# Sparse attention: one reciprocal for all head norms, compression at 128 rows, rows as head pairs, merge-gate products between the rows

## The chip, the cores and the metric

The kernel runs on one core of one Trainium2 chip. The metric is the device time of one execution in microseconds; the median of several runs is compared. PE is TensorE, DVE is VectorE, ACT is ScalarE, POOL is GpSimd, SP is SyncE, which here only issues the weight transfers.

## The reference, cut to what matters

The whole network has four transformer layers (latent attention, stick-breaking attention, retention, latent attention, each with a feed-forward part), and then one block of sparse attention with a layer of retrieved experts. The sequence has 512 tokens, the model 1024 features, everything in float32. The change touches only the sparse attention (stage "nsa"):

```
h = rms_norm(x, norm1);  z = h @ w_in
q (8 heads x 64), kc vc ks vs kw vw (2 groups x 64 each), gates, dil (3 groups x q,k,v x 4 heads x 64), mg (2 x 1024)
q, ks, kw, dil q, dil k: rms_norm over each head's 64 features, times a gain, then rotation of 16 of them
k_cmp, v_cmp = gelu(blocks(kc or vc, 32 tokens, stride 16) + pe) @ w1) @ w2      # 31 compressed tokens
per head: softmax over the compressed tokens, over the selected tokens, over a window;
          o = g0 * o_c + g1 * o_s + g2 * o_w
dilated: per head three patterns share one softmax over 3 x n keys
merged = sigmoid(mg[0]) * (y_nsa @ w_up_nsa) + sigmoid(mg[1]) * (y_dil @ w_up_dil);  x += merged @ w_o
```

At 512 tokens all key blocks are selected and the window covers all earlier tokens, so that the kernel computes both branches as causal attention.

## The kernel before, in words

Activations lie with features on the 128 partitions and 512 tokens along them. All weights come in one stream of slots of 128 x 1024 float32 (512 KB), through a ring of four: SP loads a slot when PE has released the one four before it (L351), ACT scales it in place and writes its float16 high half (L989, L992), POOL writes the low half (L438). ACT does that two slots ahead of what it evacuates (`feed`, `use`, L994 to L1006). An f32 product by weights is three f16 matmuls: high x high, high x low, low x high (`split_tile`, L486). One output tile of 128 features is one slot, 24 matmuls of 512 columns. Its PSUM bank is one of four, and is read by ACT.

The order of the sparse stage is written out by hand, as one list of instructions for each engine; semaphores join them:

1. `split_input`: norm of x, and h as two f16 halves.
2. 36 feature tiles (q, ks, kw, kc, vc, dilated q and k, and 16 tiles of the merge gate, which ACT passes through a sigmoid), then 8 slots of token-major values, then one slot for the branch gates.
3. Compression (L800 to L827): for keys and values, 2 hidden tiles each, 32 products over 64 partitions for each of the two groups, in f32 straight from the ring: 16 slots, 256 matmuls of 31 columns. Each f32 matmul is two instructions.
4. `norm_rope` (L531, L1280, L1738): 19 units (18 tiles and the compressed keys), one after the other: ACT squares, PE sums over a head's 64 partitions by a matrix of ones, ACT takes the root, DVE the reciprocal (L1490) and scales (L1433), PE turns the features by a matrix (L529), ACT copies, DVE multiplies by sine and cosine and adds.
5. `row_blocks` over 112 rows. A row is one head, one block of 128 queries and one branch: 96 branch rows (31 keys, or 128 to 512 keys twice), then 16 dilated rows with three segments each. PE makes the scores (L553), DVE adds the mask (L1574) and takes the maximum (L1580), ACT exponentiates with the sum (L1083), DVE inverts and scales (L1592, L1595), PE transposes (L569), ACT copies (L1095), PE multiplies by the values (L586). Transposes lag three rows, value products five.
6. The up-projections of both attentions, 6 slots, each multiplied by its merge gate (L1760), halved, then 8 slots of the output projection, added to x (L1768).

Of the kernel before, what the change touches and what calls it, by code (L numbers as in the profile page):

```python
# [21 lines left out]
T = 512  # L22
D = 1024
P = 128
C = D // P
# [25 lines left out]
ADA_FIRST = 2 * D  # L51
ARENA = 52
# [8 lines left out]
    "pe_k": 32, "pe_v": 32, "inv_mla": 1, "inv_ret": 1, "row_ok": 1,  # L61
# [8 lines left out]
MAT_WIDTHS = {"ident": P, "rot_mla": P, "rot_nsa": P, "pair_ones": P}  # L70
# [22 lines left out]
def build(nc, wstream, ada, ada_first, vecs, mats, phase, x_in, positions, out, stages):  # L93
# [4 lines left out]
    with ctx:  # L98
# [26 lines left out]
        small = sb("small", [P, 16])  # L125
# [3 lines left out]
        ident, rot_mla, rot_nsa, pair_ones = (mat[:, i, :] for i in range(4))  # L129
# [72 lines left out]
        s_merge = sem("merged")  # L202
        s_pe = sem("pe_added")
# [33 lines left out]
        def nsa_rows():  # L237

            rows = []
            for j in range(4):
                for g in range(NSA_G):
                    hd = 4 * g + j
                    half = slice(64 * g, 64 * g + 64)
                    for qb in range(TB):
                        q = slice(qb * P, qb * P + P)
                        n = (qb + 1) * P
                        for br in range(3):  # L250
                            if br == 0:
                                products = [(arena[half, j, q], cmp_k[half, 0:N_CMP])]
                                mask = const("nsa", "cmp_mask")[:, 32 * qb:32 * qb + N_CMP]
                                seg = Seg(products, N_CMP, mask, [(N_CMP, cmp_v[0:N_CMP, 64 * g:64 * g + 64])])
                            else:
                                products = [(arena[half, j, q], arena[half, 3 + br, 0:n])]
                                at = 128 * (br - 1) + 64 * g
                                seg = Seg(products, n, const("nsa", "causal")[:, (TB - 1 - qb) * P:T],
                                          [(P, nat(kb)[:, at:at + 64]) for kb in range(qb + 1)])
                            ok = v("row_ok") if br == 0 and qb == 0 else None  # L260
                            rows.append(Row([seg], gates[:, qb, 3 * hd + br:3 * hd + br + 1], ok,
                                            hd, qb, br == 0, br == 2,
                                            arena16[half, j] if qb == TB - 1 and br == 2 else None, 64 * g, 64))
            for hd in range(DIL_H):
                half = slice(64 * (hd % 2), 64 * (hd % 2) + 64)
                for qb in range(TB):
                    q = slice(qb * P, qb * P + P)
                    n = (qb + 1) * P
                    segs = []
                    for g in range(DIL_G):  # L270
                        at = 256 + 256 * g + 64 * hd
                        segs.append(Seg([(arena[half, 8 + 4 * g + hd // 2, q],
                                          arena[half, 10 + 4 * g + hd // 2, 0:n])], n,
                                        const("nsa", f"dil{g}")[:, (TB - 1 - qb) * P:T],
                                        [(P, nat(kb)[:, at:at + 64]) for kb in range(qb + 1)]))
                    rows.append(Row(segs, None, None, 8 + hd, qb, True, True,
                                    arena16[half, 8 + hd // 2] if qb == TB - 1 else None, 64 * (hd % 2), 64))
            return rows
# [13 lines left out]
        def nsa_units():  # L292

            cos, sin = const("nsa", "cos"), const("nsa", "sin")
            units = [(arena[:, j, :], v("nsa_q"), T, cos, sin, True) for j in range(4)]
            units += [(arena[:, 3 + i, :], v("nsa_k", i), T, cos, sin, False) for i in (1, 2)]
            for g in range(DIL_G):
                units += [(arena[:, 8 + 4 * g + i, :], v("dil_q", g), T, cos, sin, True) for i in range(2)]
                units += [(arena[:, 10 + 4 * g + i, :], v("dil_k", g), T, cos, sin, False) for i in range(2)]

            units.append((cmp_k[:, 0:N_CMP], v("nsa_k", 0), N_CMP, cos[:, 31:T:16], sin[:, 31:T:16], False))
            return units


# [29 lines left out]
        nsa_places = Places([region[:, at:at + 3, :].rearrange("p a t -> p (a t)")  # L334
                             for region, at in ((h, 0), (h, 3), (arena, 44), (arena, 49))],
# [118 lines left out]
        def _(pe):  # L454
# [70 lines left out]
            def rotate(src, stat, n=T):  # L525
                b = bank()

                wait(s_norm, "norm", 1)
                nc.tensor.matmul(b[:, 0:n], stat, src[:, 0:n], start=True, stop=True).then_inc(s_tile, 1)  # L529
# [1644 lines left out]
```

## Time and profile before

| | us |
|---|---|
| median of 3 runs | 5479.83 (5479.36 to 5482.42) |
| the profiled execution | 5478.4 |
| its span | 5476.6 |
| mean granted TensorE clock | 0.916 |
| PE busy | 4990.3 (91%) |
| DVE busy | 2244.5 (41%) |
| ACT busy | 2610.9 (48%) |
| POOL busy | 1615.8 (30%) |
| mean DMA rate | 90 GB/s |

The busy share of PE counts an instruction from its start to its end, at whichever clock, and so cannot tell whether the engine works at full speed. The granted clock does. Matmuls overlap, so the spacing of their starts is their price, not their listed duration.

### The profile page before, as it was taken

To read this page: it belongs to the slowest core of one execution; us is meant where nothing else is said; L and a number is where in the kernel's file an instruction comes from. 1 tells how busy PE (TensorE), PEld (TensorE's weight loads), DVE (VectorE), ACT (ScalarE), POOL (GpSimd) and SP (SyncE) were. 2 spreads that over 40 slices of the span, in tenths; PEclk is the share of its full clock that TensorE was granted. 3 is DMA by queue.
4 is the path that set the end of the run, shared out by engine and by line. 5 is a ranking of instruction groups with operands and counts; after the bars stand their busy time and mean duration, and the time that the engine had idled before them with its cause. 6 is when DMAs were issued, how large, how long until landed. Compare 5 with 4: busy or idle time off the path is not lost.

```text
span 5476.6 us, 69964 instructions
## 1 busy us (share of the span) xinstructions
PE 4990.3 (91%) x25520; PEld 2454.1 (45%) x25520; DVE 2244.5 (41%) x4212; ACT 2610.9 (48%) x3646; POOL 1615.8 (30%) x736
## 2 busy tenths in 40 slices
PE   3889989989989889979899997998997799999999
PEld 1444445534534434434344453455443454454444
DVE  4553022342053334044200106546298794391670
ACT  3456444566344457444664553334554444445443
POOL 1124421034323224411243341001342234334333
PEclk9889989999999999989999995558998899999999
DMA  3245311044222136310232231000232122222223
GB/s 135 97 167 211 102 62 39 24 169 180 88 68 81 66 121 229 103 47 31 69 100 88 100 106 46 1 1 24 78 103 70 62 85 93 96 86 98 92 85 103
DMA packets 124889, 493.42 MB, mean 90 GB/s; under 512 B 13872, under 2 KB 14000, under 8 KB 121248
## 3 DMA queue, kind: packets, MB, share of 16 engines
q1 hardware_dynamic: 124416, 488.31, 25.9%
q8 instruction: 123, 2.02, 0.2%
q0 software_dynamic: 288, 2.59, 0.1%
q14 instruction: 62, 0.51, 0.0%
HBM read 488.74 MB, written 2.10 MB: 90 GB/s over the span
## 4 chain that ended last, share of the span: by engine, by line
issue 49%; PE 26%; POOL 14%; DVE 11%; ACT 0%; POOLq 0%; DVEq 0%; ACTq 0%
POOL halves L438 14%; PE ps L489 6%; PE ps L490 6%; PE ps L491 6%; PE ps L553 3%; PE ps L586 2%; DVE same L1876 1%; PE ps L569 1%; DVE rows L1490 1%; PE ps L903 1%; DVE rows L1781 1%; DVE rows L1872 1%; DVE rows L1426 1%; DVE rows L1780 1%; PE ps L808 1%
## 5 line engine op out<-in xcount | busy, mean ns | idle before, releaser
L438 POOL TENSOR_TENSOR halves<-ring,halves 128x1024 f16<-128x1024 f32 x727 | 1613.6, 2220 | 3844.0 <-ACT halves L992 3843.6
L489 PE MATMUL ps<-h,halves 128*128 128x512 f16 x2912 | 1119.6, 384 | 140.3 <-DVE h L1516 127.1
L490 PE MATMUL ps<-h,halves 128*128 128x512 f16 x2912 | 1118.9, 384 | 0.0
L491 PE MATMUL ps<-h,halves 128*128 128x512 f16 x2912 | 1117.1, 384 | 0.0
L489 PE MATMUL ps<-rows,halves 128*128 128x512 f16 x2480 | 946.4, 382 | 69.9 <-DVE rows L1497 43.5
L989 ACT ACTIVATE ring<-ring 128x1024 f32<-128x1024 f32 x727 | 762.1, 1048 | 451.6 <-DMA ring<-wstream 451.2
L490 PE MATMUL ps<-rows,halves 128*128 128x512 f16 x2480 | 945.9, 381 | 0.0
L491 PE MATMUL ps<-rows,halves 128*128 128x512 f16 x2480 | 945.7, 381 | 0.0
L992 ACT ACTIVATE halves<-ring 128x1024 f16<-128x1024 f32 x727 | 768.3, 1057 | 23.1
L1490 DVE RECIPROCAL rows<-rows 128x512 f32<-128x512 f32 (+1 forms) x45 | 147.8, 3283 | 1264.0 <-ACT rows L1035 1264.0
L489 PEld LDWEIGHTS ps<-h,halves 128*128 128x128 f16 x2912 | 288.0, 99 | 499.9 <-issue 150.7
L491 PEld LDWEIGHTS ps<-h,halves 128*128 128x128 f16 x2912 | 288.2, 99 | 354.2 <-issue 18.2
L490 PEld LDWEIGHTS ps<-h,halves 128*128 128x128 f16 x2912 | 287.6, 99 | 347.6 <-issue 15.8
L489 PEld LDWEIGHTS ps<-rows,halves 128*128 128x128 f16 x2480 | 243.6, 98 | 360.6 <-DVE rows L1497 46.0
L491 PEld LDWEIGHTS ps<-rows,halves 128*128 128x128 f16 x2480 | 243.8, 98 | 296.9 <-issue 7.4
L490 PEld LDWEIGHTS ps<-rows,halves 128*128 128x128 f16 x2480 | 243.6, 98 | 283.8 <-issue 6.6
L1325 ACT ACTIVATE rows<-lasting 128x512 f32 (+1 forms) x128 | 80.7, 630 | 430.5 <-DVE lasting L1891 430.4
L553 PE MATMUL ps<-rows 64*128 64x128 f32 (+7 forms) x544 | 258.3, 586 | 26.1 <-DVE rows L1429 26.1
L1640 DVE TENSOR_TENSOR rows<-rows 128x512 f32 x128 | 88.6, 692 | 439.2 <-ACT rows L1159 439.2
L1880 DVE TENSOR_TENSOR rows<-same,scalars 128x256 f16<-128x256 f16 x512 | 241.6, 512 | 8.9
L1872 DVE TENSOR_TENSOR rows<-scalars 128x1024 f16<-128x1024 f16 x256 | 205.4, 802 | 63.4 <-PE ps L903 57.7
L1022 ACT ACTIVATE rows<-ps 128x512 f32<-128x512 f32 x156 | 90.2, 596 | 253.9 <-PE ps L491 253.5
(188 smaller groups left out, 5032.2 us busy)
## 6 DMA issues: line engine op xcount, KB each, us to landing
ring<-wstream SPq DMA_DIRECT2D x727, 512.0 KB, 3.3
rows<-ada SPq DMA_DIRECT2D x96, 768.0 KB, 4.7
rows<-ada_first SPq DMA_DIRECT2D x24, 1024.0 KB, 6.1
x<-x_in POOLq DMA_DIRECT2D x1, 2048.0 KB, 13.2
out<-x SPq DMA_DIRECT2D x8, 256.0 KB, 4.3
rows<-phase_nsa SPq DMA_DIRECT2D x1, 1600.0 KB, 6.7
rows<-phase_ret SPq DMA_DIRECT2D x1, 1024.0 KB, 4.7
rows<-positions SPq DMA_DIRECT2D x3, 256.0 KB, 5.0
```

The lines of the kernel that those rows point to most:

```text
L438: nc.gpsimd.tensor_tensor(halves[:, j % RING, 1, :], ring[:, j % RING, :], halves[:, j % RING, 0, :], ALU.subtract).then_inc(s_wlow, 1)
L489: nc.tensor.matmul(out_, high, act16[:, 0, :], start=first, stop=False)
L490: nc.tensor.matmul(out_, high, act16[:, 1, :], start=False, stop=False)
L491: return nc.tensor.matmul(out_, low, act16[:, 0, :], start=False, stop=last)
L553: mm = nc.tensor.matmul(ps[:, g % 3, 0:sg.keys], a, b, start=(k == 0), stop=(k == len(sg.products) - 1))
L586: mm = nc.tensor.matmul(o, va, pt[s][0:nk, kb * P:kb * P + P], start=(r.start and k == 0), stop=(r.stop and k == len(todo) - 1))
L989: nc.scalar.activation(ring[:, at % RING, :], ring[:, at % RING, :], ACT.Copy, scale=W_SCALE).then_inc(s_wscaled, 1)
L992: nc.scalar.activation(halves[:, at % RING, 0, :], ring[:, at % RING, :], ACT.Copy).then_inc(s_whigh, 1)
L1022: nc.scalar.activation(dst, b, func, scale=scale / W_SCALE).then_inc(s_evac, 1)
L1490: link(nc.vector.reciprocal(buf[:, 0:n], buf[:, 0:n]))
L1872: nc.vector.tensor_tensor(hot1[:, n].rearrange("p t (e o) -> p t e o", o=2), key_pairs(0, P, pairs), token_pairs(buf, 0, n, pairs), ALU.is ...
L1880: last = nc.vector.tensor_tensor(hot2[:, n, a, :].rearrange("p (t e o) -> p t e o", t=8, o=2), same_, token_pairs(buf, 2 + a, n, part_pair ...
```

## The change

- Slots: 68 in the stage and not 76. The order is now 20 feature tiles, 4 token slots, 8 compression slots, the small product, 4 token slots, branch gates, 16 merge-gate tiles, 6 + 8 as before.
- Norms: ACT squares each tile as it reads it from PSUM, and applies gain and scale in the same pass; PE adds the squares' sums of all 18 tiles into one bank of 36 rows (`stat`); one root, one reciprocal of 36 x 512. For each tile PE then makes two f32 products (`turn`): the turned features, and the inverse norms spread over the partitions; DVE multiplies, adds, and scales out of PSUM (`roped`). The turns are put between token slots and compression tiles. The compressed keys have a norm of their own at the end.
- Compression: ACT lays two neighbouring tokens on top of each other, so that a product runs over 128 partitions; position terms are added and the sum halved to f16; 24 f16 matmuls of 62 columns (both groups) a slot.
- Rows: two heads side by side (`pair_rows`), 48 branch pairs, then 8 dilated pairs. Mask, maximum and sign are one DVE instruction. Transposes lag two pairs (dilated: one), value products one more. Two banks take transposes where three did.
- Between the branch pairs PE makes the 16 merge-gate tiles (`fill`, 128 triples of matmuls, two or three for each pair), ACT copies them; the 16 sigmoids stand behind all rows.

```diff
-            "nsa": 4 + 4 + 12 + 16 + 8 + 1 + 16 + 1 + 4 + 2 + 8, "peer": 8 + 1 + 256}[stage[0]]
+            "nsa": 20 + 4 + 8 + 1 + 4 + 1 + 16 + 6 + 8, "peer": 8 + 1 + 256}[stage[0]]
...
+        MG_BANK = 7
+        FILL = ((1, 1), (2, 1), (2, 1))
...  PE
+            def pair_rows(pairs, places, fill):
...
+                        for s in range(len(pairs[i][0].segs)):
+                            for row in pairs[i]:
+                                sg, g = row.segs[s], seen["seg"] - base_seg
+                                if g >= 3:
+                                    pe.wait_ge(s_masked, base_mask + g - 2)
+                                a, b = sg.products[0]
+                                nc.tensor.matmul(ps[:, g % 3, 0:sg.keys], a, b, start=True, stop=True)\
...
+                    fill(i, 0)
+                    if lag <= i < n + lag:
...
+                                if s == 0:
+                                    pe.wait_ge(s_normed, base_row + 2 * (i - lag) + c + 1)
+                                if g - base_pt >= 2:
+                                    pe.wait_ge(s_ptc, base_ptc + g - base_pt - 1)
...
+                    fill(i, 1)
+                    if i >= lag + 1:
...
+                        pe.wait_ge(s_ptc, seen["ptc"])
...
+                def stat(m):
+                        wait(s_sq, "sq", 1)
+                        mm = nc.tensor.matmul(ps[0:STATS, 6, :], window[:, STATS - 2 * u:2 * STATS - 2 * u],
+                                              y[:, u % 4, :], start=(u == 0), stop=(u == UNITS - 1))
...
+                def turn(u, src, n):
...
+                    if u >= 2:
+                        pe.wait_ge(s_rope, u - 1)
+                    nc.tensor.matmul(ps[:, 4 + u % 2, 0:n], rot_nsa, src, start=True, stop=True)
+                    lo = P * (u % UNITS)
+                    nc.tensor.matmul(ps[:, 6 + u % 2, 0:n], spreads[:, lo:lo + P], y[0:STATS, 5, 0:n], start=True, stop=True)\
...
+                        b = bank()
+                        for late in range(2):
+                            w = slot()
+                            for t in range(8):
+                                mm = split_tile(b[:, 0:2 * N_CMP].rearrange("p (g c) -> p g c", g=NSA_G), w,
+                                                slice(t * P, t * P + P), src[:, :, :, late:late + N_CMP, t],
+                                                late + t == 0, late == 1 and t == 7)
+                            mm.then_inc(s_used, 1)
+                        some_turns(2)
...
+                tokens(lambda s: some_turns((3, 2, 2, 0)[s]))
...
+                    for _ in range(FILL[i % 3][place]):
+                        m, k = next(units)
+                        if k == 0:
+                            if m:
+                                pe.wait_ge(s_mg, m)
+                            slot()
+                        mm = split_tile(ps[:, MG_BANK, :], (mg0 + m) % RING, slice(k * P, k * P + P), h16[:, k],
+                                        k == 0, k == C - 1)
...  ACT
+                        nc.scalar.activation(y[:, u % 4, :], b, ACT.Square, scale=1.0 / W_SCALE).then_inc(s_sq, 1)
+                        nc.scalar.activation(arena[:, m, :], b, ACT.Identity, scale=unit_gains[u]).then_inc(s_evac, 1)
...
+                    if i % 3 == 0 and 1 <= i // 3 <= 16:
+                        m = i // 3 - 1
+                        use(1)
+                        nc.scalar.activation(arena[:, 28 + m, :], ps[:, MG_BANK, :], ACT.Copy,
...
+                pair_rows(nsa_pairs(), nsa_places, merge_gate)
+                pair_rows(dil_pairs(), dil_places, lambda i: None)
+                for m in range(8):
+                    for gate in (28 + m, 36 + m):
+                        nc.scalar.activation(arena[:, gate, :], arena[:, gate, :], ACT.Sigmoid).then_inc(s_sig, 1)
...  DVE, in its own pair_rows: all segments of pair i, then the scaling of pair i - 1
+                                nc.vector.tensor_tensor_reduce(
+                                    out=probs(places, rw)[:, at:at + sg.keys],
+                                    in0=ps[:, (seen["seg"] - 1 - base_seg) % 3, 0:sg.keys], in1=sg.mask, scale=-1.0,
+                                    scalar=3.0e38 if s == 0 else low, op0=ALU.add, op1=ALU.min, accum_out=low)\
...
+                def roped(u, chunk, cos_, sin_, n):
+                    link(mul(y[:, 6, 0:n], ps[:, 4 + u % 2, 0:n], sin_))
+                    link(mul(chunk, chunk, cos_))
+                    link(add(chunk, chunk, y[:, 6, 0:n]))
+                    mul(chunk, chunk, ps[:, 6 + u % 2, 0:n]).then_inc(s_rope, 1)
```

## Rows read from the trace of the kernel before

**Rows 1.** The page's second part: the granted clock in 40 equal slices of the span.
```profile
PEclk9889989999999999989999995558998899999999
```

**Rows 2.** Stage by stretches: us; busy us and instructions of each engine; clock; DMA.
```profile
3025.00:3217.00 192.00, 190.36 (x875) 85.92 (x876) 9.30 (x15) 97.46 (x113) 79.11 (x37) 0.99 0.30 99
3217.00:3265.00 48.00, 44.92 (x279) 22.95 (x277) 0.00 (x0) 20.69 (x24) 18.47 (x9) 1.00 0.26 88
3265.00:3322.00 57.00, 54.55 (x531) 53.82 (x528) 0.00 (x0) 38.07 (x46) 34.22 (x17) 0.52 0.47 158
3322.00:3441.00 119.00, 74.54 (x76) 19.16 (x76) 110.51 (x94) 35.91 (x61) 2.12 (x1) 0.50 0.01 4
3441.00:3701.00 260.00, 258.94 (x749) 144.54 (x750) 127.79 (x407) 83.27 (x295) 0.00 (x0) 0.50 0.00 1
3701.00:3790.00 89.00, 84.41 (x476) 61.30 (x476) 54.48 (x94) 37.45 (x84) 0.00 (x0) 0.88 0.00 1
3790.00:3877.00 87.00, 76.22 (x341) 33.93 (x339) 40.84 (x49) 33.72 (x36) 30.23 (x14) 0.94 0.24 79
```

**Rows 3.** Instructions in order of time, DVE, one unit of the norms: start, us.
```profile
3330.81 3.35 DVE L1490 RECIPROCAL rows<-rows 128x512 f32<-128x512 f32 x1 [0.75 <-ACT rows L1035]
3334.20 0.75 DVE L1433 SCALAR_TENSOR_TENSOR rows<-rows,lasting 128x512 f32<-128x512 f32 x1
3335.05 1.42 DVE L1426 TENSOR_TENSOR rows<-rows 128x512 f32<-128x512 f32 x2
...
3337.11 3.35 DVE L1490 RECIPROCAL rows<-rows 128x512 f32<-128x512 f32 x1
```

**Rows 4.** Order of time, PE at full clock: f16 and f32 of 512 columns.
```profile
3876.20 0.38 PE L491 MATMUL ps<-h,halves 128*128 128x512 f16 x1
3876.41 7.03 PE L482 MATMUL ps<-rows,lasting 128*128 128x512 f32 x16
```

**Rows 5.** Groups of 3265:3322: count, busy us, mean ns, idle before.
```profile
L808 PE MATMUL ps<-rows,ring 64*128 64x31 f32 x512 | 52.9, 386 | 0.7 <-POOL halves L438 0.7
...
L438 POOL TENSOR_TENSOR halves<-ring,halves 128x1024 f16<-128x1024 f32 x17 | 36.1, 2126 | 27.2 <-ACT halves L992 27.2
L992 ACT ACTIVATE halves<-ring 128x1024 f16<-128x1024 f32 x17 | 18.0, 1057 | 0.5
L989 ACT ACTIVATE ring<-ring 128x1024 f32<-128x1024 f32 x17 | 17.9, 1055 | 13.4 <-DMA ring<-wstream 13.4
```

**Rows 6.** Order of time, PE in the gate slot, 128 columns.
```profile
3264.80 0.22 PE L496 MATMUL ps<-halves,h 128*128 128x128 f16 x1
3264.86 0.22 PE L497 MATMUL ps<-halves,h 128*128 128x128 f16 x1
```

**Rows 7.** Order of time, PE in the branch rows, half clock.
```profile
3501.51 1.54 PE L586 MATMUL ps<-rows 128*64 128x128 f32 x6
3502.98 0.79 PE L553 MATMUL ps<-rows 64*128 64x128 f32 x2
3503.71 0.69 PE L569 MATMUL ps<-lasting,rows 128*128 128x128 f32 x2
```

**Rows 8.** Order of time, PE in the dilated rows, full clock.
```profile
3743.79 2.20 PE L553 MATMUL ps<-rows 64*128 64x384 f32 x6
3745.92 1.53 PE L569 MATMUL ps<-lasting,rows 128*128 128x128 f32 x12
```

**Rows 9.** Groups of DVE and ACT in 3441:3701, then of ACT in 3730:3786.
```profile
L1574 DVE TENSOR_TENSOR rows<-ps,rows 128x512 f32<-128x512 f32 x16 | 11.1, 692 | 35.7 <-PE ps L553 35.7
L1580 DVE TENSOR_REDUCE small<-rows 128x1 f32<-128x512 f32 x16 | 11.0, 686 | 0.5
...
L1083 ACT ACTIVATION_READ_ACCUMULATOR rows<-rows,small 128x1 f32 x48 | 9.0, 187 | 0.0
...
L1083 ACT ACTIVATE rows<-rows,small 128x1536 f32<-128x1536 f32 x3 | 4.7, 1576 | 10.0 <-DVE small L1580 10.0
L1095 ACT ACTIVATE rows<-ps 128x512 f32<-128x512 f32 x8 | 4.3, 595 | 0.0
```

**Rows 10.** Stretches in the dilated rows and in the expert stage.
```profile
3720.00:3740.00 20.00, 18.92 (x121) 14.14 (x121) 14.85 (x26) 10.49 (x26) 0.00 (x0) 1.00 0.00 1
4189.00:4369.00 180.00, 150.63 (x1452) 78.44 (x1450) 133.12 (x315) 73.78 (x94) 46.80 (x22) 0.91 0.20 65
```

More of the change, by code:

```diff
@@ L51 @@
 ADA_FIRST = 2 * D
+UNITS = 18
+STATS = 2 * UNITS
 ARENA = 52
@@ L235, in mla_rows, with nsa_pairs @@
             return rows
-        def nsa_rows():
-            rows = []
+        def nsa_pairs():
+            pairs = []
             for j in range(4):
[L244 to L265, printed above, removed]
                 for qb in range(TB):
@@ L523, in linear_tokens @@
                         mm.then_inc(s_used, 1)
[L525 to L529, printed above, removed]
-            def norm_rope(units):
-                for i in range(len(units) + 1):
-                    if i < len(units):
-                        sum_squares([tmp[:, 0:units[i][2]]], pair_ones, units[i][2])
-                    if i:
-                        rotate(units[i - 1][0], rot_nsa, units[i - 1][2])
             def row_blocks(rows, places):
@@ new lines, in nsa, with some_turns @@
+                turns = iter(range(UNITS))
+                def some_turns(n):
+                    for _ in range(n):
+                        u = next(turns)
+                        turn(u, arena[:, unit_rows[u], :], T)
+                for m in range(20):
+                    b = bank()
+                    w = slot()
+                    for k in range(C):
+                        if m == 0:
+                            wait(s_hlow, "hlow", 1)
+                        mm = split_tile(b, w, slice(k * P, k * P + P), h16[:, k], k == 0, k == C - 1)
+                    mm.then_inc(s_used, 1)
+                    if m >= 2:
+                        stat(m - 2)
@@ new lines, in tokens @@
+                def tokens(after):
+                    banks = [bank() for _ in range(TB)]
+                    for s in range(4):
+                        w = slot()
+                        for tb in range(TB):
+                            for k in range(2):
+                                mm = split_tokens(banks[tb], w, slice(k * T, k * T + T), h16[:, 2 * s + k],
+                                                  slice(tb * P, tb * P + P), s + k == 0, s == 3 and k == 1)
+                        mm.then_inc(s_used, 1)
+                        after(s)
@@ L1105, in row_blocks @@
                 seen["pv"] += len(rows)
+                seen["mask"] += sum(len(row.segs) for row in rows)
             def mla():
@@ L1260, in nsa @@
+                for tb in range(TB):
+                    tokens_copy(arena[:, 21 + 2 * tb, :], tb)
+                feed(seen["used"] + 1 + AHEAD)
+                roots(N_CMP)
                 b = tile(1)
```

431 lines of the change are left out of this document (310 added, 121 removed).

## The prediction

> **What bounds the kernel now.** I read the page first: TensorE's (PE's) clock row shows that the engine ran at half speed for three slices and part of a fourth in the middle [rows 1]. Those are the sparse-attention stage, the only one that the change touches. I then cut that stage by its loops [rows 2]. Its seven stretches are 36 feature tiles; 8 token slots and a gate slot; the compression; the head norms with rotation; 96 branch rows; 16 dilated rows; the merge. The clock column matters most: 1.00 in the first two, then 0.50 from the compression to the first dilated rows, so that some 450 us run at 1.2 GHz instead of 2.4.
>
> Each stretch has its own limit. In the first two it is PE's 24 matmuls of a slot. In the compression PE issues narrow matmuls. In the norms it is VectorE (DVE), busy 110.5 of 119 us. In the branch rows PE is busy 258.9 of 260 us, with DVE at 128 and ScalarE (ACT) at 83. Weight feeding binds nowhere: GpSimd's (POOL's) difference costs 2.1 us a slot.
>
> **Head norms: one reciprocal.** One unit takes 6.3 us, from reciprocal to reciprocal: 3.35 for the reciprocal, the rest scaling and rotation [rows 3]. 18 such units plus a short one fill the 119 us. After, squares come from ACT while tiles are read, PE gathers their sums in one bank, and one reciprocal on 36 partitions serves all; 512 elements a partition cost 3.35 us whatever the partition count, I assume. Per unit DVE keeps four passes of about 0.71 us (1.42 for two, [rows 3]), 2.85 us. The 18 sum 51 us, and lie beside the first token slots, the compression and the second token slots. PE pays, in place of the DVE path, 18 sum matmuls and 36 for turn and spread. A full f32 matmul of 512 columns is two instructions, 16 in 7.03 us, 0.43 each [rows 4]: 18 x 0.86 = 15.5 us and 36 x 0.86 = 31.0 us, all now on PE's path.
>
> **Compression at 128 rows.** Before: 512 instructions, PE busy 52.9 us, 3.3 us a slot over 16 slots; 57 us with the small products and the wait around them [rows 2, 5]. After: 8 slots of 24 f16 matmuls with 62 columns. The nearest row is the gate slot's, 128 columns every 0.055 us [rows 6], so 1.3 us a slot, 10.6 us in all; at the old price per instruction, 0.104, it would be 20. Eight turns (13.8 us) sit between them, and DVE allows one each 2.85 us. The feed needs 2.1 us on ACT and 2.1 on POOL [rows 5], beside that. At full clock that is 26 us for slots and turns together. But the old compression lost the clock at its very start (0.52 on the mean of its stretch, 1.00 just before, [rows 2]), and PE will wait for feeds here too; at 1.2 GHz a turn takes 3.4 us, 8 x 3.4 + 10.6 = 38. I take 32, with 22 and 40 as ends.
>
> **Everything ahead of the rows.** A dense slot is 24 matmuls at 0.216 us [rows 4], 5.18 us. Before: 45 such slots = 233 us, plus 6 us of slow start and bank waits, is the first two stretches (239 us, from PE's start at 3026); with 57 and 119 the rows began after 415 us. After: 29 slots = 150, slow start 6, sums 15.5, compression with its turns 32, the ten other turns 17.2, waits of turns for DVE 3, a slow start of the second token slots 2, two small products 2, the compressed keys' own norm and rotation at the end 3: 231 us. **Gain 184 us.** But 16 slots of it, 83 us, are only moved.
>
> **Branch rows as pairs, with the moved products.** Columns streamed by 12 rows before: scores 2684, each four passes (two instructions, [rows 7]); 24 transposes of two passes; 24 value products of four. At 1.2 GHz that is 8.9 + 5.1 + 10.2 = 24.3 us, 195 us for 96 rows; the stretch took 260, so 0.68 us a row is change-over between kinds. It shows in [rows 7]: the score product starts 0.73 us ahead of its follower, where 0.43 stream. At 2.4 GHz streaming halves to 97 us. The change-over there is about 0.2 for one kind (six instructions of 384 columns stream 1.92 and the next kind starts after 2.13, [rows 8]). A pair has one change-over set for two rows, 48 x 0.7 = 34. The 128 filled triples cost 128 x 0.65 = 83. Sum 214 us; some change-overs hide under the 512-column fills, for which I take off 9: **205 us, gain 55.** Ends: 176 if the halves of the array overlap (below), 247 if nothing hides and a pair pays for both rows (34 more).
>
> DVE and ACT hide: the fused mask-max replaces add (0.69) and reduction (0.69) at 512 keys [rows 9]. The before shows no such instruction; its ends are one pass, 0.69, and both, 1.4. Even at 1.4 DVE stays under 130 us of 205. ACT has 83 us of row work plus 16 slots of feed and copy at 2.7, 126 us; the copy waits for a tile that PE finished one step earlier, so exponentials behind it do not starve PE.
>
> The Trainium skill, TensorEngine Tiling, Key Properties, says that tiles of the array run independently and that changing the tiling drains the engine. The second half agrees with the 0.2 to 0.3 us at [rows 7, 8]; the first would favour the change more than I book, and is a rival below.
>
> **What clock.** At the end of the dilated rows PE had gone back to full clock by itself (1.00 in 3720:3740) though two engines wait in turn there [rows 10]. The branch rows now start behind five dense slots, and have dense fills in each step, no wait for DVE: I take full clock.
>
> **Dilated rows.** No fills, three segments, and a lag of one pair where before it was three rows. Here waits are added. PE's transposes of pair i-1 stand behind the scores of pair i, and wait for a DVE scaling that stands behind all six mask-max of pair i; ACT's copies stand behind the two exponentials of pair i. At 512 keys: scores 5.1, then two exponentials of 1.58 + 0.19 and latency before copies run, 4.5; six copies of 0.59 through two banks, 3.5; value products 5.1 [rows 9]. Over the four sizes: 13.6 + 11.9 + 10.5 + 12.8 = 49 us for two heads, 98 for four. Before it was 89, of which some 20 at the lower clock (0.88 on the mean, [rows 2]). I add 4, for parts of it at the lower clock: **102 us, loss 13.** Ends: 84 (value products overlapped) and 150 (lower clock throughout: streaming doubles from 64 to 128, part of the waits vanish); with mask-max at 1.4, 15 more.
>
> **Merge.** The 16 sigmoids move behind the rows, 0.6 each like ACT's copies [rows 9], ahead of the feed of the third merge slot. That slot is ready 9.5 + 2.1 + 2.1 us and latency after the rows, PE wants it after 10.4: **loss 5** (0 to 8).
>
> **Sum.** -184 - 55 + 13 + 5 = -221 us. The profiled execution took 5478.4 us (span 5476.6); 5257. Its time is 1.4 below the median of 5479.83, which gives 5259; forecast 5260. Other stages keep their instructions.
>
> **Rivals.**
> - *The heads' halves overlap in the array.* Alternating rows 0-63 and 64-127, and alternating output halves, let one matmul run during its neighbour. For: neighbours in issue order now differ in half. Against: each f32 matmul is two instructions on one half, and in the old compression, which alternated too, 0.104 us per instruction is twice what 31 columns stream [rows 5]. Half of the value products' 41 us and a quarter of the scores' 36 would hide, 29; in the dilated rows half of 26, 13: 5260 - 42 = 5218.
> - *Lower clock in compression and dilated rows only.* For: narrow matmuls lost the clock before; PE waits over 4 us a step in the dilated rows. Against: the expert stage, PE busy 151 of 180 us with regular waits, averages 0.91 [rows 10]. +45 and +6: 5311.
> - *Lower clock through both row stretches (slower side).* The fills run at half speed as well: 128 x 3 x 0.427 = 164, with 195 streamed and 38 of change-over: 397 against 260 before; all of the compression and its turns +10; dilated 150. -184 + 10 + 137 + 61 + 5 = +29: 5509. It decides once the clock is lost for more than about 85% of the rows. For: before, PE was busy 100% there and the clock stayed low for 260 us [rows 2]. Against: the dense fills, and the full clock at the entry.
> - *A queue wait.* Turns bunched before the compression or mask-max at two passes tie PE to DVE: +30, 5290. The fused operation then saves nothing.
>
> **Chances.** Forecast 56% (its own range 5230 to 5290), overlap 18%, partial lower clock 14%, queue wait 6%, lower clock throughout 6%. Range 5195 to 5335. A measurement of this kernel tells 0.2%, 11 us, from no change: faster 0.94, same 0.01, slower 0.05.
>
> **What would show it.** Clock 1.00 from the first slot to the end of the branch rows; rows starting 231 us after PE's start; 48 pairs in 205 us with 16 dense tiles inside; 17 fewer long reciprocals; dilated pairs with PE idle behind ACT copies; PE idle once, some 5 us, at the third merge slot. The forecast is wrong if the clock row shows half speed in the branch rows, if the mask-max costs far over 0.69 us, or if the turns pace the compression.

## The result, and the profile after

The changed kernel takes 5266.96 us (median of 4 runs, 5263.86 to 5267.79), the kernel before 5480.33 (5479.36 to 5482.42): ratio 0.9609 [0.9592, 0.9626], 213 us faster. The forecast was 5260, range 5195 to 5335. The profiled execution has a span of 5265.0 us and a mean clock of 0.943 (before 0.916).

The granted clock in 40 slices, to be held against [rows 1]: the three slices at half speed are gone; of this stage one slice is at 0.7, the 25th, which holds the compression.

```profile
PEclk8889989999989998997999997989998999999999
```

The stage by stretches, the counterpart of [rows 2] (us; busy us and instructions of PE, PEld, DVE, ACT, POOL; clock; DMA share; GB/s). They are the feature tiles with the first token slots; the compression with eight turns; the second token slots with seven turns and the gate slot; 48 branch pairs with the 16 merge tiles; 8 dilated pairs; the merge.

```profile
3029.00:3181.00 152.00, 151.34 (x625) 59.84 (x626) 26.34 (x29) 77.48 (x100) 53.44 (x24) 0.99 0.26 83
3181.00:3234.00 53.00, 53.00 (x225) 29.31 (x224) 28.36 (x34) 17.03 (x20) 17.94 (x8) 0.55 0.25 80
3234.00:3285.00 51.00, 46.85 (x243) 21.57 (x242) 26.46 (x37) 18.51 (x24) 13.34 (x6) 0.90 0.17 53
3285.00:3484.00 199.00, 173.99 (x1152) 92.58 (x1152) 97.63 (x397) 119.52 (x341) 35.35 (x16) 0.97 0.14 45
3484.00:3575.00 91.00, 74.76 (x456) 49.05 (x456) 37.27 (x130) 38.16 (x82) 0.00 (x0) 0.76 0.00 1
3575.00:3663.00 88.00, 74.42 (x337) 33.37 (x338) 40.64 (x49) 42.91 (x53) 30.16 (x14) 0.94 0.24 78
```

By PE's starts, against the steps of the prediction:

| us | before | forecast | after | missed by |
|---|---|---|---|---|
| ahead of the rows | 415.6 | 231 | 256.0 | +25 |
| branch rows | 253.3 | 205 (from a stretch called 260) | 199.5 | -1 in the gain (54, forecast 55) |
| dilated rows | 95.6 (called 89) | 102 | 90.1 | -18.5 in the change (-5.5, forecast +13) |
| merge | 86.1 | +5 | 88.1 | -3 |

I had cut before the first dilated score at 3701 and it starts at 3694.7, so I compare changes there, not totals. The rest of the run moved by 1 to 5 us. The total missed by only 7 us, but two misses of 25 and 18.5 us ahead of the rows and in the dilated rows stand in it against each other.

In the compression PE is busy for all of its 53 us at a clock of 0.55, where I had forecast 32. A slot of 62 columns there (first fence, PE in order of time) starts an instruction every 0.113 us, at full clock already (the granted clock fell only at 3185.6), where I had taken 0.055 from [rows 6]. A turn (second fence; two products of two instructions each) takes 2.0 to 2.1 us from start to next start at full clock, ahead of the compression, and 4.0 within it, at half clock.

```profile
3181.99 0.29 PE L507 MATMUL ps<-rows,halves 128*128 128x62 f16 x1
3182.10 0.29 PE L508 MATMUL ps<-rows,halves 128*128 128x62 f16 x1
3182.21 0.29 PE L509 MATMUL ps<-rows,halves 128*128 128x62 f16 x1
```

```profile
3176.87 1.02 PE L872 MATMUL ps<-rows,lasting 128*128 128x512 f32 x2
3177.82 1.12 PE L874 MATMUL ps<-rows 36*128 36x512 f32 x2
3178.88 1.12 PE L872 MATMUL ps<-rows,lasting 128*128 128x512 f32 x2
...
3188.32 2.07 PE L874 MATMUL ps<-rows 36*128 36x512 f32 x2
3190.33 2.07 PE L872 MATMUL ps<-rows,lasting 128*128 128x512 f32 x2
```

The branch rows hit their number, but not its terms. What PE waits for there (the view of waits, 3285:3484), then ACT in order of time at one of the first waits (PE stood still for 1.6 us there, until 3303.15):

```profile
PE ps L507 <- ACT rows L1494: 22.6, 15, 1.9
PE ps L818 <- ACT rows L1424: 1.4, 1, 1.4
PE ps L802 <- DVE rows L1632: 1.1, 1, 1.1
```

```profile
3300.42 0.41 ACT L1424 ACTIVATE rows<-ps 31x128 f32<-31x128 f32 x2
3300.73 1.04 ACT L1137 ACTIVATE ring<-ring 128x1024 f32<-128x1024 f32 x1
3301.80 1.06 ACT L1140 ACTIVATE halves<-ring 128x1024 f16<-128x1024 f32 x1
3302.77 0.58 ACT L1494 ACTIVATE rows<-ps 128x512 f32<-128x512 f32 x1
```

All 16 merge tiles go through one bank. The next tile waits until ACT has read it (L1494), and ACT first prepares a slot of weights, 2.1 us (L1137, L1140). I had given the fills no wait at all.

### The profile page after: what moved, and what is told of

It reads as the page before. It is cut to its first block, busy times and chain, and to the rows that moved or that the text cites. A ratio compares the mean times of both kernels' runs of the same rounds, so it can differ in the third digit from the quotient of the medians.

```text
span 5265.0 us, 69183 instructions
## 1 busy us (share of the span) xinstructions
PE 4786.4 (91%) x25238; PEld 2319.2 (44%) x25238; DVE 2159.1 (41%) x4231; ACT 2578.9 (49%) x3607; POOL 1600.4 (30%) x728
## 4 chain that ended last, share of the span: by engine, by line
issue 56%; PE 20%; POOL 14%; DVE 9%; POOLq 0%; ACT 0%; DVEq 0%; ACTq 0%
POOL halves L456 14%; PE ps L507 6%; PE ps L508 6%; PE ps L509 6%; DVE same L2151 1%; DVE rows L2056 1%; PE ps L1051 1%; DVE rows L2147 1%; DVE rows L2055 1%; DVE rows L2155 1%; DVE rows L2058 1%; DVE rows L1632 0%; DVE rows L1635 0%; DVE rows L2096 0%; DVE rows L2099 0%
## 5 line engine op out<-in xcount | busy, mean ns | idle before, releaser
L507 PE MATMUL ps<-rows,halves 128*128 128x512 f16 (+1 forms) x2544 | 965.5, 380 | 72.1 <-DVE rows L1703 43.5
L1137 ACT ACTIVATE ring<-ring 128x1024 f32<-128x1024 f32 x719 | 753.7, 1048 | 444.0 <-DMA ring<-wstream 443.4
L508 PE MATMUL ps<-rows,halves 128*128 128x512 f16 (+1 forms) x2544 | 965.3, 379 | 0.0
L509 PE MATMUL ps<-rows,halves 128*128 128x512 f16 (+1 forms) x2544 | 964.8, 379 | 0.0
L1140 ACT ACTIVATE halves<-ring 128x1024 f16<-128x1024 f32 x719 | 759.8, 1057 | 22.8
L1696 DVE RECIPROCAL rows<-rows 128x512 f32<-128x512 f32 x26 | 87.2, 3352 | 1075.4 <-ACT rows L1183 1075.4
L507 PEld LDWEIGHTS ps<-rows,halves 128*128 128x128 f16 x2544 | 251.4, 99 | 368.5 <-DVE rows L1703 46.0
L509 PEld LDWEIGHTS ps<-rows,halves 128*128 128x128 f16 x2544 | 251.8, 99 | 297.1 <-issue 7.9
L508 PEld LDWEIGHTS ps<-rows,halves 128*128 128x128 f16 x2544 | 251.6, 99 | 284.0 <-issue 7.0
L1523 ACT ACTIVATE rows<-ps 128x512 f32 (+1 forms) x128 | 76.4, 597 | 274.2 <-PE ps L509 274.0
L500 PE MATMUL ps<-h,lasting 128*128 128x512 f32 x272 | 154.7, 720 | 52.9 <-ACT h L1177 52.6
## 6 DMA issues: line engine op xcount, KB each, us to landing
out<-x SPq DMA_DIRECT2D x8, 256.0 KB, 4.5
rows<-positions SPq DMA_DIRECT2D x3, 256.0 KB, 4.9
```

The costliest lines, as they stand in the source:

```text
L500: mm = nc.tensor.matmul(b[:, 0:n], ones[:, :] if stat is None else stat, sq, start=(k == 0), stop=(k == len(squares) - 1))
L507: nc.tensor.matmul(out_, high, act16[:, 0, :], start=first, stop=False)
L508: nc.tensor.matmul(out_, high, act16[:, 1, :], start=False, stop=False)
L509: return nc.tensor.matmul(out_, low, act16[:, 0, :], start=False, stop=last)
L1137: nc.scalar.activation(ring[:, at % RING, :], ring[:, at % RING, :], ACT.Copy, scale=W_SCALE).then_inc(s_wscaled, 1)
L1140: nc.scalar.activation(halves[:, at % RING, 0, :], ring[:, at % RING, :], ACT.Copy).then_inc(s_whigh, 1)
```

## The experiments

Every run is given with its ratio to the kernel before; "changed kernel" is 5266.96.

**e1: the compressed operand without steps.**

```diff
-  raw = arena[:, 6 + kind, :].rearrange("p (c s) -> p c s", s=8)
+  raw = arena[:, 6 + kind, :].rearrange("p (g c s) -> p g s c", g=NSA_G, s=8)
...
-  src[:, :, :, late:late + N_CMP, t],     # step of 8 elements
+  src[:, :, :, t, late:late + N_CMP],     # neighbours
```

> The compressed operand is laid out so that the 62 columns of a compression matmul are two runs of neighbouring elements instead of two runs with a step of eight. In the changed kernel such a matmul took 0.113 us, at either granted clock, against 0.055 us for a 128-column one of the gate slot. Theory A (the step of the moving operand sets the 0.113): the matmuls fall to about 0.055, the stage from 53.4 to about 35 us, the kernel gets 10 to 20 us faster. Theory B (the 0.113 is the price of loading the weights for so few columns, or of writing them): spacing stays at 0.34 for three, stage and kernel stay within 3 us. I hold B at 0.55, since at half clock the spacing did not change, which a load of the engine itself should.

5248.38 us (5242.05 to 5263.19), 0.9586 [0.9573, 0.9599]. Theory A, which I had held the less likely. The order of elements is changed where DVE writes the operand and where PE reads it. PE in order of time, and two stretches of the compression:

```profile
3188.53 0.24 PE L507 MATMUL ps<-rows,halves 128*128 128x62 f16 x1
3188.58 0.24 PE L508 MATMUL ps<-rows,halves 128*128 128x62 f16 x1
3188.63 0.24 PE L509 MATMUL ps<-rows,halves 128*128 128x62 f16 x1
3188.68 0.24 PE L507 MATMUL ps<-rows,halves 128*128 128x62 f16 x1
...
3190.86 2.06 PE L872 MATMUL ps<-rows,lasting 128*128 128x512 f32 x2
```

```profile
3178.00:3181.00 3.00, 3.00 (x52) 1.98 (x52) 2.93 (x4) 2.95 (x4) 2.63 (x2) 1.00 0.24 64
...
3186.00:3208.00 22.00, 19.76 (x164) 10.12 (x164) 20.74 (x21) 9.58 (x12) 13.16 (x6) 0.73 0.31 101
```

With nothing changed but the order of elements in memory the spacing falls from 0.113 us to 0.052 at half clock (above), and to 0.030 in the first slot, at full clock (first stretch of the next fence): 192 times 0.06 to 0.08 is 12 to 16 us. From the first of these matmuls to the first row it is 84.2 us and not 104.2; the rest goes with a higher clock and so cheaper turns. The branch rows gave 2.9 back, at a clock of 0.95 against 0.97 and with the same idle time.

**e7: e1, and no turns in the compression.**

```diff
-                        some_turns(2)            # after each compression tile
...
-                tokens(lambda s: some_turns((3, 2, 2, 0)[s]))
+                tokens(lambda s: some_turns((4, 4, 4, 3)[s]))
```

> On top of the neighbouring layout of the compressed operand, the eight turns leave the compression, and all of the fifteen still open stand in the second token slots. Theory A (the compression loses the clock whatever stands between its narrow matmuls, which idle behind weight feeding: 8 slots of 1.25 us against 2.1 us of feeding): clock at 0.5 to 0.8 in it all the same, about 20 us long, and the turns then tie the token slots to VectorE's 2.85 us each, 15 by 2.85 = 43 us and more: kernel 5 to 20 us slower than with the layout alone (5248). Theory B (the f32 turns take the clock): full clock in the compression. Then the turns' place costs less, within 5 us of 5248.

5271.12 us (5269.50 to 5274.79), 0.9621 [0.9608, 0.9634], 23 over e1. Theory A, somewhat beyond its range. The narrow matmuls alone, with the idle time between their slots (PE busy 10.9 of 22 us), bring the clock to 0.61. Of what it costs in the token slots, some 12 us are PE waiting for DVE, which theory A had named (7.6 us at the turns and 4.2 behind them, against 0.8 in e1); the rest goes with the clock, which averages 0.75 from the end of the compression to the first row (0.94 in e1); at half clock a turn takes 4.0 us. The compression and the start of the token slots:

```profile
3178.00:3200.00 22.00, 10.91 (x207) 9.71 (x203) 5.87 (x5) 18.89 (x25) 17.59 (x9) 0.61 0.60 199
3200.00:3220.00 20.00, 17.12 (x40) 5.51 (x40) 9.90 (x12) 5.99 (x6) 8.43 (x4) 0.76 0.13 45
```

So the place of the turns in the change is worth having, and the half clock in the compression does not need them. Why the changed kernel loses it although PE is never idle there is not settled by this: in e1, with idle gaps and shorter matmuls, the clock was higher (0.73 from its second slot on) than in the changed kernel (0.55).

**e4: no fills; the merge tiles dense, ahead of the rows.**

```diff
+                for m in range(16):
+                    if m >= 4:
+                        pe.wait_ge(s_mg, m - 3)
+                    slot()
+                    for k in range(C):
+                        mm = split_tile(ps[:, 4 + m % 4, :], ...)
+                    mm.then_inc(s_used, 1)
+                pe.wait_ge(s_mg, 16)
-                pair_rows(nsa_pairs_, nsa_places, fill)
+                pair_rows(nsa_pairs_, nsa_places, lambda i, place: None)
```

> The 16 merge-gate tiles are computed densely ahead of the branch rows, not between them; same work. They take 16 tiles by 2.1 us, 34 us, at full clock. Theory A (the fills hold the clock at 0.97 in the rows, which without them falls to about 0.5): the rows take about 200 to 250 us behind the 34, the kernel gets 50 to 90 us slower. Theory B (the rows' own work holds the clock once they are entered at full clock): rows about 170 us, together about 205 against 199.5, kernel 0 to +15 us. Theory C (the waits for the single merge bank cost more than the fills hide): kernel faster by up to 10 us. I hold A at 0.5, B at 0.35, C at 0.15.

The 34 us in that text is my slip: a tile is 24 matmuls, 5.2 us, and 16 are the 83 us that the prediction uses. 5260.66 us (5256.44 to 5263.86), 0.9597 [0.9585, 0.9610]. The tiles take 84.0 us, the rows 113.6, together 197.6 against 199.5. Stretches of the tiles, and of the rows in three parts:

```profile
3286.00:3369.00 83.00, 82.53 (x383) 37.22 (x381) 0.00 (x0) 40.25 (x47) 34.05 (x16) 1.00 0.30 98
3369.00:3400.00 31.00, 26.61 (x168) 15.23 (x168) 20.84 (x108) 20.43 (x78) 0.00 (x0) 0.78 0.06 18
3400.00:3440.00 40.00, 35.26 (x296) 21.43 (x294) 30.55 (x154) 29.55 (x116) 0.00 (x0) 0.96 0.01 2
3440.00:3482.00 42.00, 35.26 (x308) 22.33 (x306) 29.76 (x135) 29.34 (x102) 0.00 (x0) 0.96 0.00 1
```

Theory A falls: without fills the rows keep 0.78 to 0.96 of the clock. As the change places them the fills gain nothing; what they hide they lose again at the single bank. The kernel is 6 us faster, which is theory C by a little, but only 2 of the 6 lie in the tiles and branch rows, and the two intervals overlap.

**e5: ACT copies the merge tile before it prepares the next slot.**

```diff
                     if i % 3 == 0 and 1 <= i // 3 <= 16:
                         m = i // 3 - 1
-                        use(1)
+                        seen["used"] += 1
+                        act.wait_ge(s_used, seen["used"])
                         nc.scalar.activation(arena[:, 28 + m, :], ps[:, MG_BANK, :], ACT.Copy, ...)
+                        feed(seen["used"] + AHEAD)
```

> ScalarE copies a finished merge tile out of its single bank before it prepares the next slot of weights, not after (the preparation is 2.1 us). In the changed kernel TensorE waits 22.6 us in 15 waits for that copy. Theory A (the wait is this order): it all but goes, branch rows 199.5 to about 180, kernel 15 to 22 us faster. Theory B (the wait is turned into another, since TensorE, VectorE and ScalarE hand the rows round): under 6 us. The kernel with the tiles computed densely ahead of the rows had none of these waits and its rows with the tiles took 197.5 us, which speaks for B; I hold it at 0.6.

5238.18 us (5235.28 to 5239.66), 0.9557 [0.9544, 0.9570]: 29 us faster than the changed kernel. Theory A, and more than its 15 to 22 us: PE's idle time in the branch rows falls by 22 (25.5 to 3.2), and the same instructions take 6 us less at a clock of 1.00 and not 0.97. PE's wait for the copy in the branch rows is 0.3 us, and PE has no gap:

```profile
3285.00:3330.00 45.00, 44.65 (x296) 23.44 (x294) 22.35 (x111) 29.98 (x92) 8.52 (x4) 1.00 0.15 48
3330.00:3380.00 50.00, 50.00 (x351) 26.91 (x349) 25.12 (x123) 36.08 (x107) 10.64 (x5) 1.00 0.17 54
3380.00:3430.00 50.00, 50.00 (x342) 26.78 (x341) 25.32 (x122) 35.42 (x103) 10.63 (x5) 1.00 0.16 54
```

The branch rows take 171.3 us and not 199.5. Against e4's 197.6 the interleaving is worth 26 us once its queue is in order. My argument for B, from e4, was wrong: e4 has no fills to hide its own 16 us of idle time.

**e2: the mask-max as two instructions again.**

```diff
-  nc.vector.tensor_tensor_reduce(out=..., in0=ps..., in1=sg.mask, op0=ALU.add, op1=ALU.min, accum_out=low)
+  nc.vector.tensor_tensor(..., ps..., sg.mask, ALU.add)         # per segment
+  nc.vector.tensor_reduce(out=low, in_=..., op=ALU.max, negate=True)   # once per row
```

> The fused mask-max is undone: a masked add per segment and one maximum over the row, as in the kernel before; the rest stays. Theory A (VectorE has slack in the branch rows, and is a link only in the dilated rows): the branch rows stay within 3 us of 199.5, the dilated rows get 5 to 20 us longer than 90.1, kernel +5 to +23 us. Theory B (VectorE is never the link): kernel within 3 us. Theory C (the branch rows hang on it as well, as my rival of the mask-max at two passes did the other way round): branch rows 20 us or more longer.

5311.52 us (5308.18 to 5359.83), 0.9709 [0.9681, 0.9736]: 45 us slower than the changed kernel. Theory C, and with it A for the dilated rows. Branch rows 229.4 us (+29.9), dilated rows and merge +14.4. DVE is still idle nearly half of the time in the branch rows, but PE's wait at the bank has grown, and the clock has fallen from 0.97 to 0.87. By PE's starts 12 of the 30 us are more idle time, and 18 are the same instructions taking longer. The stretch of the branch rows, then the wait:

```profile
3285.00:3514.50 229.50, 191.86 (x1152) 100.97 (x1152) 122.53 (x398) 123.58 (x341) 33.99 (x16) 0.87 0.12 39
```

```profile
PE ps L507 <- ACT rows L1494: 33.4, 15, 3.2
```

**e13: two instructions, and the copy first** (the edits of e2 and e5).

> Both edits together: ScalarE copies the merge tile first (that alone took the kernel to 5238, its branch rows to 171.3 us) and the mask-max is two passes again (that alone took it to 5311, branch rows 229.4). Theory A (the two passes cost through the single merge bank: each later exponential delays the copy behind it, and TensorE waits 33.4 us for copies there): with the copy first, the branch rows come to 171 to 185, kernel 5250 to 5265. Theory B (VectorE's longer chain paces the rows themselves): branch rows stay 195 to 205, kernel 5275 to 5290. I hold A at 0.5.

5261.85 us (5258.94 to 5263.19), 0.9601 [0.9588, 0.9614]. Theory A. Branch rows 182.3 us: with the queue in order the two passes cost 11.0 us there, not 29.9: 10 of idle time and 1 of streams, since the clock stays at 0.99. The other 19 came only with the copy behind the preparation, 17 of them as the lower clock. Behind the branch rows, where there are no fills, the two passes cost much the same either way, 14.4 and 12.8 us. The stretch of the branch rows, then the wait at the bank:

```profile
3284.40:3466.60 182.20, 168.98 (x1152) 91.45 (x1152) 122.54 (x397) 120.85 (x341) 34.02 (x16) 0.99 0.15 50
```

```profile
PE ps L507 <- ACT rows L1495: 9.2, 12, 1.1
```

**e3: value products head after head.**

```diff
-                        for k, (s, kb) in enumerate(todo):
-                            for c, row in enumerate(pair):
+                        for c, row in enumerate(pair):
+                            for k, (s, kb) in enumerate(todo):
```

> The value products of a pair are issued head after head and not alternately; same instructions, same count. In the changed kernel sixteen alternating ones took 1.03 to 1.09 us, 0.065 each, against 0.115 for one before. Theory A (alternation between the two halves of the output columns lets them run beside each other): they go back to 0.11 each, some 0.75 us for each of about 80 groups, which would be up to 60 us of TensorE time, of which the slack of the rows hides a part: +10 to +40 us. Theory B (0.065 is the price of the shape alone, in any order): within 3 us.

5277.16 us (5275.67 to 5281.07), 0.9629 [0.9617, 0.9642]: 10 over the changed kernel, the low end of theory A; +1.6 in the branch rows, +8.3 behind them.

**e12: the same, with the copy first** (the edits of e3 and e5), so that PE is the link.

> Both edits together: the merge tile is copied first, so that TensorE is busy all the time in the branch rows (50.0 of 50 us), and the value products are issued head after head. With waits around them that order cost 1.6 us in the branch rows. Theory A (TensorE had slack then, the overlap of the halves is worth 384 products by 0.03 to 0.05 us where it is the link): branch rows 171 to 185 or more, kernel 12 to 25 us over 5238. Theory B (the overlap is worth little): within 6 us of 5238.

5249.78 us (5247.86 to 5255.55), 0.9579 [0.9566, 0.9592]: 12 over e5, the low end of A again; +4.1 in the branch rows, +7.3 behind them. Twelve products of a pair, then what follows them, PE in order of time, in e5 (first) and here:

```profile
3441.54 0.88 PE L837 MATMUL ps<-rows 128*64 128x128 f32 x12
3442.34 1.13 PE L802 MATMUL ps<-rows 64*128 64x512 f32 x4
```

```profile
3449.85 1.14 PE L837 MATMUL ps<-rows 128*64 128x128 f32 x12
3450.92 1.13 PE L802 MATMUL ps<-rows 64*128 64x512 f32 x4
3451.98 0.39 PE L507 MATMUL ps<-h,halves 128*128 128x512 f16 x1
```

0.80 us against 1.07. Eight products take 0.59 in either order, so that only rows with more keys gain. One such product took 0.12 us before, so eight would be 0.9: by this count they overlap head after head as well, and the edit takes away only a part of the overlap.

**e6: in the dilated rows the scaling of pair i-1 ahead of the mask-max of pair i.**

```diff
                 for i in range(n + lag + 3):
+                    if early and 1 <= i < n + 1:
+                        scale_pair(i)
                     if i < n:
...
-                    if 1 <= i < n + 1:
+                    if not early and 1 <= i < n + 1:
```

> In the dilated rows VectorE scales the probabilities of pair i-1 before the six mask-max of pair i, not behind them. TensorE waits 12.4 us for that scaling there. Theory A (the order costs what the wait shows): dilated rows 90.1 to about 80, kernel 5 to 12 us faster. Theory B (the scaling then waits for the exponential with the mask-max queued behind it, scores come later): 0 to +6 us. I hold A at 0.5.

5266.01 us (5262.30 to 5267.08), 0.9609 [0.9596, 0.9622]: nothing, outside theory A (5 to 12 us) and next to B. The wait changed its name: in the changed kernel (first) PE's transposes wait for DVE's scaling, here for ACT's copies.

```profile
PE ps L818 <- DVE h L1973: 7.5, 7, 2.4
PE ps L818 <- DVE rows L1973: 4.9, 4, 1.6
```

```profile
PE ps L818 <- ACT rows L1424: 16.4, 13, 3.1
```

**e10: a faster version, with dense tiles** (the edits of e1, e4 and e6, and the sigmoid reads the bank itself):

```diff
-                    nc.scalar.activation(arena[:, 28 + m, :], ps[:, 4 + m % 4, :], ACT.Copy, ...)
+                    nc.scalar.activation(arena[:, 28 + m, :], ps[:, 4 + m % 4, :], ACT.Sigmoid, ...)
```

> A version made to beat the changed kernel: the compressed operand in neighbouring elements, the 16 merge tiles computed densely ahead of the rows, each read out of its bank by the sigmoid itself (no sigmoids behind the rows), and the scaling of the dilated rows ahead of the mask-max. From the parts: -18 (layout), -6 (dense tiles), -5 for the wait at the third merge slot and the table load, 0 to -10 for the scaling: 5267 - 34 = 5233, range 5222 to 5245. If the parts don't add, because the clock in the rows falls with less dense work before them, 5250.

5241.13 us (5238.02 to 5242.73), 0.9562 [0.9549, 0.9575]. In its range (5222 to 5245), 8 us above the sum of the parts. From the first dilated score to the experts it is 173.8 us against 178.2, so that the sigmoids behind the rows cost the change some 4 at most.

**e11: a faster version, with fills** (the edits of e1 and e5, and slots prepared between the sigmoids).

```diff
                         nc.scalar.activation(arena[:, gate, :], arena[:, gate, :], ACT.Sigmoid).then_inc(s_sig, 1)
+                    if m in (1, 3):
+                        feed(seen["used"] + AHEAD + (m + 1) // 2)
```

> A version made to beat the changed kernel: neighbouring layout of the compressed operand, merge tile copied first, and the slots behind the rows prepared between the sigmoids rather than behind all of them. From the parts: 5267 - 18.6 - 28.8 - 4 = 5216, range 5205 to 5230. If the clock falls in the rows, 5235.

5220.94 us (5211.13 to 5224.25), 0.9524 [0.9511, 0.9537]: 46 us faster than the changed kernel. The parts add up to within 5 us (5216 expected). Compression and branch rows:

```profile
3182.00:3212.00 30.00, 25.08 (x218) 12.12 (x217) 28.47 (x29) 17.23 (x19) 18.65 (x8) 0.76 0.30 106
...
3267.00:3437.00 170.00, 166.81 (x1156) 89.91 (x1156) 83.70 (x396) 118.03 (x341) 34.10 (x16) 1.00 0.16 53
```

**e9: e11 with another placing of the fills** (`FILL = ((0, 2), (2, 1), (2, 1))`).

> As the version of neighbouring layout, copy first and slots between the sigmoids, and of every three pairs the first has both its fills ahead of the value products and none ahead of the transposes (FILL (0,2) for (1,1)), so that the merge tile which ends the three gets more time until its copy. Theory A (a rest of the wait for the copy is left, 0.3 us): nothing, within 3 us of it. Theory B (transposes then wait for the scaling with no dense work between): 5 to 15 us slower.

5221.60 us (5212.91 to 5223.27), 0.9526 [0.9513, 0.9539]: no difference, theory A.

## Why the prediction was right, and where its steps were not

The clock came back, and the two large gains are where they were put. That the total is within 7 us is in part luck: the misses of the stretches stand against each other, and so do those inside the branch rows.

**Ahead of the rows: the direction right, 25 us short.** The step that failed is "the nearest row is the gate slot's, 128 columns every 0.055 us". That row's operand lies in neighbouring elements, the compressed operand in steps of eight; e1 shows that the step makes the price two to four times as high. My other end, 0.104 per instruction, would have been the better value. The second part is the clock, which I had as an end (40 us) and not as the forecast, and a turn, 2.1 us and not 1.72 at full clock, 4.0 at half: 8 x 24 x 0.113 + 8 x 4.0 = 54 for the measured 53.4, 21 of the 25 us. The other ten turns took 21.5 us for 17.2; why a turn costs more than the 16 equal products of [rows 4] is not shown. The sums took 18.1 for 15.5, and smaller terms went the other way. (The 26 us that the prediction gives for slots and turns at full clock are 24.4 by its own terms; nothing hangs on them.) The single reciprocal did what it says: on 36 partitions it took 3.35 us, as on 128, which was an assumption, and the run has 17 fewer of them.

**Branch rows: the number right, two terms wrong by nearly the same amount.** I take PE's time from start to next start, idle time off, summed over the stretch: scores 31.4, transposes 22.9, value products 28.7, fills 91.0, idle 25.5, together 199.5. Forecast: 97 of streams and 34 of change-over less 9, which is 122 for the rows' own work, and 83 for fills, no idle. So the rows' own work was 83 and not 122, the fills took 8 more, and PE waited 25 us that the sum did not have. The cause of the first is most likely the rival that I gave 18%, the halves of the array. At full clock six score instructions of 512 columns on one half took 2.77 us in the kernel before, 0.46 each (below). A pair's four, two heads on different halves, take 1.06 us, 0.27 each (3450.92 to 3451.98 in e12, above). Value products: 0.12 each before at full clock, 0.067 in groups of twelve.

```profile
3748.84 2.84 PE L553 MATMUL ps<-rows 64*128 64x512 f32 x6
3751.61 0.55 PE L569 MATMUL ps<-lasting,h 128*128 128x128 f32 x3
```

I had priced the overlap as half of the value products and a quarter of the scores, 29 us. If half of both is hidden it is 38, and the miss of 39 is accounted for with the change-overs as forecast; that is an estimate. An edit shows only a part of it: by e3 and e12 the order within the value products is worth 4 us in the branch rows and 7 to 8 behind them. The scores were not tried in another order, so their share is read from rows alone. The Trainium skill says in TensorEngine Tiling (Array Packing), Key Properties, that tiles of the array run independently. This case now agrees for alternating heads (0.27 us against 0.46). I had weighed against it that an f32 product is two instructions on one half, and that is no hindrance. My other argument, that the old compression alternated halves and took 0.104 us an instruction all the same, is not answered by any run.

The second is the step "ACT and DVE hide": "the copy waits for a tile that PE finished one step earlier, so exponentials behind it do not starve PE". I had looked at what stands behind the copy, not at the 2.1 us ahead of it, nor at who waits for the bank. e5 shows it worth 28 us in the rows. From the same step: "even at 1.4 DVE stays under 130 us of 205" is true as a sum (122.5 busy in e13) and wrong as a conclusion; a second pass costs 30 us in the branch rows (e2), 19 of which go when the copy comes first (e13). My rival of a queue wait named DVE, and was priced from the mask-max, which took 0.69 us at 512 keys as forecast; the queue that did wait was ACT's. And that rival's price, 30 us for the whole kernel, was too low: e2 is 45 us slower.

**Clock.** Full speed in the branch rows as forecast (0.97), but not for the reason given, that dense fills hold it: e4 has none and averages 0.91. What does hold it is not shown; in the kernel before PE was busy for 258.9 of 260 us at half clock there, and no run here enters the changed rows at half clock. In the dilated rows it was 0.76, lower than forecast.

**Dilated rows: wrong in sign, 18 us.** The waits that I foresaw are there (PE idle 16 us, behind DVE's scaling and ACT's copies), and in e6 taking the one away brings out the other. The step that failed is "Before it was 89": the stretch starts at 3694.7 and took 95.6 us, which is 6.6 of the miss. The other 12 are in the sum, 102 for 90.1. Value products took 18.5 us where it has 25.6, the overlap that I had left to the rival (in e3 it is worth 8 us behind the branch rows). Transposes and idle time together took 42.9 for 44.8, and scores 28.7 for 27.2, so that no overlap shows in these scores; the 4 us added for a lower clock can't be told apart.

**Merge:** +2, forecast +5. PE's wait at the third merge slot is there, but is 2.8 us and not 5; e10 bounds what the sigmoids cost at 4.

## What to carry to other kernels

Before a duration is borrowed from another row, compare the layout of its operands too, not only type and column count: a step of eight made a matmul two to four times as dear. Where work is slipped into the gaps of another loop, walk its buffer round once, from the engine that fills it to the one that empties it, with all that stands ahead of the emptying instruction in its queue; an engine with much idle time can still be the link. And a forecast that comes out right is to be opened as one that comes out wrong: here 39 us too much for PE's own work hid 34 too little for waits and fills, and the wait, once seen, gave a kernel that is 29 us faster.

## What the runs showed of the hardware that was not expected

- An f16 matmul of 62 columns is issued every 0.113 us where the moving operand has a step of eight elements (16 bytes), at full and at half clock, as if the clock did not bear on it. Where the elements are neighbours it is 0.030 us at full clock and 0.052 at half (e1), and so follows the clock.
- Alternating f32 scores of two heads on array rows 0 to 63 and 64 to 127: 0.27 us per instruction of 512 columns against 0.46 on one half.
- Value products head after head cost as much as alternating ones up to eight in a row (0.59 us), more from twelve on (1.07 against 0.80). On one half alone such a product took 0.12 us before.
- The fused mask-max at 512 keys takes 0.69 us, as long as the add alone did before ([rows 9]), with a read of the accumulator of 0.08 us behind it:

```profile
L1948 DVE CUSTOM_DVE_ANT_0 rows<-ps,rows 128x512 f32<-128x512 f32 x16 | 10.4, 689 | 27.9 <-PE ps L802 27.9
L1948 DVE DVE_READ_ACCUMULATOR2_ANT small<- 128x1 f32 x96 | 8.0, 83 | 0.2 <-issue 0.2
```
